# The first key group's convolution by halves of the batches between the gathers, and two gate blocks inside the sample's selected attention

## What is computed

```python
def compress(k, pe, w1, w2):                      # kcb, vcb: compressed blocks
    chunks = ...                                  # 16 tokens x 64 channels each
    pre = pe.reshape(-1) @ w1                     # position term
    for j in range(2):
        pre = pre + jnp.einsum('bngf,fh->bngh', chunks[:, j:j + n_cmp], w1r[j])
    return jax.nn.gelu(pre) @ w2

def merge_branches(o_nsa, o_hg, ga, gb, w_branch_a, w_branch_b, w_out):
    m = jax.nn.sigmoid(ga) * (o_nsa @ w_branch_a) + jax.nn.sigmoid(gb) * (o_hg @ w_branch_b)
    return m @ w_out

# sample: past = cache_cmp[page_table]; kcb, vcb = compress(past + new); top-16 blocks of 64 tokens are
# gathered from cache_sel for o_slc; o_win attends state_win and the new tokens; new_win_sample is
# state_win shifted by the 4 new tokens
```

## Time and profile before

| | |
|---|---|
| median of 3 runs | 1476.8 us (1475.82 to 1482.26) |
| the profiled execution | 1477.04 us, of it 1475.2 us span of the core |
| mean granted clock of TensorE | 0.954 |
| PE busy | 1292.9 us (88%), PEld 639.3 us (43%) |
| DVE, ACT, POOL busy | 397.5 us (27%), 257.1 us (17%), 32.1 us (2%) |
| chain that ended last, by engine | PE 64%, DMA 26%, DVE 3%, SPq 2% |
| convolution of 504 columns (L811), all | 56.8 us busy, 256 records |
| gate blocks (L1220), all | 67.8 us busy, 256 records |

### The profile page before, as it was taken

The page is one execution under the profiler, slowest core; times in us unless marked ns, Lnnn a source line. Parts: engine busy times, 40 slices in busy tenths (PEclk is TensorE's granted clock), DMA queues, the critical chain, the costliest instruction groups (busy, mean ns, idle before and its releaser), DMA issues.

```text
span 1475.2 us, 32485 instructions
## 1 busy us (share of the span) xinstructions
PE 1292.9 (88%) x14329; PEld 639.3 (43%) x14329; DVE 397.5 (27%) x991; ACT 257.1 (17%) x618; POOL 32.1 (2%) x50
## 2 busy tenths in 40 slices
PE   5899998799989978899999679999998669797685
PEld 4554555466767433344444224444443123242232
DVE  5320012458743551112121102121211011121012
ACT  5100005556520310001010001010100000000001
POOL 2000003100000000000000000000000000000000
PEclk9899999999999989899999989999999789899897
DMA  9985764224297999999999999699999999999996
GB/s 283 328 305 200 265 231 168 68 60 156 61 260 254 377 378 424 424 423 426 426 424 422 425 425 425 273 420 414 424 424 425 422 425 425 426 422 424 426 425 252
DMA packets 99043, 503.98 MB, mean 342 GB/s; under 512 B 9473, under 2 KB 38937, under 8 KB 63938
## 3 DMA queue, kind: packets, MB, share of 16 engines
q1 hardware_dynamic: 95234, 483.47, 82.4%
q0 software_dynamic: 3520, 18.90, 3.7%
q10 hardware_dynamic: 192, 0.13, 0.0%
HBM read 496.33 MB, written 10.31 MB: 343 GB/s over the span
## 4 chain that ended last, share of the span: by engine, by line
PE 64%; DMA 26%; DVE 3%; SPq 2%; ACT 2%; issue 1%; POOL 0%; DVEq 0%; ACTq 0%
PE psum L1444 18%; DMA arena<-in_w_up 12%; DMA arena<-in_w_down 11%; PE psum L1463 9%; PE psum L811 4%; PE psum L1220 3%; PE psum L1051 3%; PE psum L1052 3%; PE psum L1477 3%; PE psum L1416 2%; PE psum L1317 2%; PE psum L1430 2%; DMA arena<-in_cache_cmp,arena 2%; SPq L702 2%; PE psum L824 1%
## 5 line engine op out<-in xcount | busy, mean ns | idle before, releaser
L1444 PE MATMUL psum<-arena 128*32 128x512 f32 x3328 | 407.3, 637 | 110.3 <-DMA arena<-in_w_up 95.2
L1444 PEld LDWEIGHTS psum<-arena 128*32 128x32 f32 x3328 | 114.8, 113 | 371.2 <-issue 288.2
L2493 DVE TENSOR_SCALAR arena<-psum 128x256 f32<-128x256 f32 x52 | 22.2, 426 | 678.6 <-PE psum L1430 678.6
L1463 PE MATMUL psum<-arena 128*32 128x256 f32 x3328 | 192.7, 381 | 7.7 <-DMA arena<-in_w_down 7.7
L1463 PEld LDWEIGHTS psum<-arena 128*32 128x32 f32 x3328 | 101.6, 110 | 75.7 <-DMA arena<-in_w_down 12.8
L1880 ACT ACTIVATE arena<-arena 128x256 f32<-128x256 f32 x52 | 21.7, 418 | 572.7 <-DVE arena L2493 572.7
L1220 PE MATMUL psum<-arena 128*128 128x288 f32 x256 | 67.8, 410 | 3.5 <-DMA arena<-in_w_in 2.9
L1477 PE MATMUL psum<-arena 32*128 32x256 f32 x864 | 61.9, 399 | 1.1 <-ACT arena L1889 0.6
L811 PE MATMUL psum<-arena 64*128 64x504 f32 x256 | 56.8, 598 | 1.7 <-DVE arena L1959 1.7
L1430 PE MATMUL psum<-arena 32*32 32x512 f32 x416 | 57.6, 625 | 0.0
L1416 PE MATMUL psum<-arena 128*32 128x256 f32 x832 | 55.9, 386 | 0.0
(11 more groups left out here) (458 smaller groups left out, 1319.5 us busy)
## 6 DMA issues: line engine op xcount, KB each, us to landing
arena<-in_w_up SPq DMA_DIRECT2D x128, 2048.0 KB, 31.7
arena<-in_w_down SPq DMA_DIRECT2D x64, 2048.0 KB, 26.4
arena<-in_w_ada SPq DMA_DIRECT2D x12, 2048.0 KB, 11.3
arena<-in_w_in SPq DMA_DIRECT2D x6, 2048.0 KB, 12.0
arena<-in_w_in SPq DMA_DIRECT2D x16, 512.0 KB, 4.1
arena<-in_state_win SPq DMA_DIRECT2D x4, 1024.0 KB, 11.0
arena<-in_w_out SPq DMA_DIRECT2D x1, 4096.0 KB, 18.1
out<-in_state_win SPq DMA_DIRECT2D x1, 4064.0 KB
```

What stands on the lines that cost most here:

```text
L1444: last = mm(banks[0][32 * j:32 * j + SLOT].rearrange("p (h c) -> p h c", h=2), xcT[:, q % 2, q // 2], up_cols[n % R_][:, q % 2, j], start= ...
L1463: last = mm(banks[1][32 * j:32 * j + SLOT, 256:512], aT[:, v, 2 * m + h], down_cols[n % R_][:, h, v, j], start=m + v + h == 0, stop=m + v ...
```

## The change

1. `convolve` takes a range of batches. Banks 4 and 5 (`block_bank`) hold group 0; they are first written by two matmuls of `prow`, which is still zero at that point, so that all later ones accumulate. The transposes of a batch become `raw_to_kvT(b)`. Group 0's first 16 positions run for batches 0 to 3 between the transposes of batches 5, 6 and 7, then for batches 4 to 7, then positions 16 to 31 for all, and only then come the rows, the modulations 0 to 2 and the rest. The front modulations use banks 0 and 1.
2. The first 16 positions of `w1` are issued by ScalarE at the program's start, the others and `w2` by SP behind the prompt's rows; these wait for `landed[6]`. The first slab of `w_in` waits for the last front modulation's copy (`mod_v`).
3. Two gate blocks (`EARLY`) leave the planned part: block 0 stands in place of `keep_clock` ahead of the selected probabilities, block 1 in four pieces in the loop. They have banks 2 and 4 and buffers of their own and wait for `s_max`. ScalarE's tanh for them stand in the same part. Their columns of `w_in` are those of the last two blocks (`gate_column`), so that the planned blocks keep their columns. `INSIDE` is now blocks 2 to 11, at the same places among the prompt's steps, `LEFT` is 12 to 15.
4. SP issues the loads of blocks 0 and 1 when the window values are through (`pv_ps` 2). The loop over the later loads starts at block 2; the copy of `state_win` stands behind `load_gate(5)` as before.

```diff
+EARLY = 2
+def gate_column(j):
+    return (j - EARLY) % NGATE
...
+AHEAD = EARLY + len(INSIDE)
...
-            for v in range(2):
-                sp.dma_start(w1[DH * v:DH * v + DH], A["cmp_w1"][0, v].rearrange("(s d) h -> d s h", d=DH)).then_inc(S("ld_w1"), 16)
...
-            sp.wait_ge(S(landed[5]), 16)
+            sp.wait_ge(S(landed[6]), 16)
...
+            sp.wait_ge(S("ld_w1"), 32)
+            for v in range(2):
+                sp.dma_start(w1[DH * v:DH * v + DH, 16:32], block_weights(v)[:, 16:32]).then_inc(S("ld_w1"), 16)
...
+            def load_gate(j):
+                if j >= EARLY + 2:
+                    sp.wait_ge(S("gate_ps"), j - 1)
+                c0 = ZW + P * gate_column(j)
+                sp.dma_start(piece_of(j), w_in[:, c0:c0 + P].rearrange("(k p) c -> p k c", p=P)).then_inc(S(f"ld_gp{j % 2}"), 16)
+
+            sp.wait_ge(S("pv_ps"), 2)
+            for j in range(EARLY):
+                load_gate(j)
             sp.wait_ge(S("pv_ps"), 3)
...
-            for j in range(min(NGATE, len(INSIDE) + 2)):
+            for j in range(EARLY, min(NGATE, AHEAD + 2)):
                 load_gate(j)
                 if j == 5:
...
+            for v in range(2):
+                mm(block_bank(0, v)[:, 0:NB * NCMP], prow[0:32, v], ident[0:32, 0:1].broadcast_to([32, NB * NCMP]), start=True, stop=False)
+            for b in range(6):
+                raw_to_kvT(b)
+            for q in range(4):
+                pe.wait_ge(S(f"pair_out{q}"), 4)
+            pe.wait_ge(S("ld_w1"), 32)
+            convolve(0, 0, 8, 0, 4)
+            raw_to_kvT(6)
+            convolve(0, 8, 16, 0, 4)
+            raw_to_kvT(7)
...
-            pe.wait_ge(S("ld_w1"), 48)
-            convolve(0, 0, 16)
-            after(pe, "peT")
+            convolve(0, 0, 16, 4, NB)
+            pe.wait_ge(S("ld_w1"), 80)
+            convolve(0, 16, 32)
             for n in range(3):
                 rows_to_hT(n)
                 modulation(n)
-            convolve(0, 16, 32)
             position_terms()
...
-                if (what, n) == ("sel_p", 0):
-                    keep_clock(bank, 10)
...
+            pe.wait_ge(S("mod_v"), FRONT)
...
+            def early_gate(j, ks):
+                if ks[0] == 0:
+                    pe.wait_ge(S(f"ld_gp{j % 2}"), 16)
+                    pe.wait_ge(S("s_max"), 4)
+                for k in ks:
+                    last = mm(banks[2 + 2 * j][:, 0:TP + NS], piece_of(j)[:, k], hT[:, k], start=k == 0, stop=k == KD - 1)
...
+            early_gate(0, range(KD))
             for t in range(5):
                 probs_T("sel_p", t, 3)
+                if t < 4:
+                    early_gate(1, range(2 * t, 2 * t + 2))
                 if t:
                     cached_values("sel_p", t - 1)
...
+            for v in range(2):
+                act.dma_start(w1[DH * v:DH * v + DH, 0:16], block_weights(v)[:, 0:16]).then_inc(S("ld_w1"), 16)
...
             for t in range(5):
                 probs_out("sel_p", t, 2)
+            gates_out(0)
             act.wait_ge(S("pv_ps"), 3)
             nc.scalar.copy(o_ev[:, 0], banks[0][:, 0:P]).then_inc(S("oS"), 1)
+            gates_out(1)
```

More of the change, by code:

```diff
@@ L242 @@
 _end = max(n for n, s in enumerate(PROMPT_STEPS) if s[0] not in ("gates", "gates_out"))
-INSIDE = [j for j in range(NGATE) if PROMPT_STEPS.index(("gates_out", (j,))) < _end]
-LEFT = [j for j in range(NGATE) if j not in INSIDE]
+INSIDE = [j for j in range(EARLY, NGATE) if PROMPT_STEPS.index(("gates_out", (j,))) < _end]
+LEFT = [j for j in range(EARLY, NGATE) if j not in INSIDE]
+AHEAD = EARLY + len(INSIDE)
 PROMPT_STEPS = [s for s in PROMPT_STEPS if s[0] not in ("gates", "gates_out") or s[1][0] in INSIDE]
@@ L775, in rows_to_hT, with raw_to_kvT @@
                 last.then_inc(S("hT_ps"), 1)
-            for b in range(NB):
+            def raw_to_kvT(b):
                 pe.wait_ge(S(landed[b]), 16)
@@ L809, in convolve @@
                         half = slice(DH * v, DH * v + DH)
-                        src = kvT[half, g, s % 16].rearrange("p (b c) -> p b c", c=64)[:, :, s // 16:s // 16 + NCMP]
-                        last = mm(banks[2 * g + v][:, 0:NB * NCMP], w1[half, s], src, start=s == 0, stop=s == 31)
+                        src = kvT[half, g, s % 16].rearrange("p (b c) -> p b c", c=64)[:, b0:b1, s // 16:s // 16 + NCMP]
+                        last = mm(block_bank(g, v)[:, NCMP * b0:NCMP * b1], w1[half, s], src, start=g == 1 and s == 0, stop=s == 31)
                 if past == 32:
@@ L1219, in gate_block @@
                 for k in range(4 * half, 4 * half + 4):
-                    last = mm(banks[7][:, 0:TP + NS], gate_piece[j % 2][:, k], hT[:, k], start=k == 0, stop=k == KD - 1)
+                    last = mm(banks[7][:, 0:TP + NS], piece_of(j)[:, k], hT[:, k], start=k == 0, stop=k == KD - 1)
                 if half:
```

55 lines of the change are left out of this document (30 added, 25 removed).

## The result

The changed kernel takes 1488.97 us (median of 4 runs, 1486.62 to 1491.79) against 1476.45 us before: 12.5 us more; the ratio is 1.0089 (13.1 us) with a 95% interval of 1.0058 to 1.0120. The forecast was 1482.9 with a range up to 1488.5; the direction was right, the size was half of what came, and the time lies 0.5 us above the range. The profiled execution took 1486.6 us (span 1484.8) and is the shortest of the four, 9.6 us over the profiled one of before. The other 2.9 us lie between the profiled executions and the medians; the other three runs had a mean granted clock of 0.945 to 0.948, the profiled one 0.953, and where they lost it no trace here shows.

What follows compares the result with a forecast made beforehand. The expert-weight stream bounds the kernel and starts when the merged rows mT are done, so TensorE's path there counts. 1477.0-1.6-3.5+11.0 = 1482.9 us; own range 1479 to 1486.5, wider range 1474 to 1488.5.

Steps and rivals of the forecast that it cites:

- Part 2: Two early gate blocks at the selected softmax and its loop, two fewer behind the prompt: -3.5 us, bounds -6 and -1.
- Part 3: Copy of the window state issued two blocks earlier in the prompt's steps; TensorE waits for columns: +11.0 us, bounds 6.5 and 13.
- ScalarE's and VectorE's lead: During TensorE's wait behind the copy both run ahead, worth about 1 us of their later waits, bounds 0 and 3.
- Rival (a): Prompt's steps: the columns behind the copy don't wait for it, giving 1471.9 us; chance 0.11.
- the loads beside the last gather: Early gates' column loads issued beside batch 7's gather of selected rows: +0.3 us, bounds 0 and 3.
- The loop: Behind the selected softmax, second early block spread over it: 4.2 us less 0.32 us of waits, +3.9.
- the end: Behind the prompt: two blocks out, -8.4, most of 2.9 us waits gone, 1.4 left, +1.9 for VectorE's sums.
- new wait for VectorE's sums: Behind the prompt TensorE waits for eight sums of state that two fewer blocks no longer cover: +1.9 us.
- Part 1: Group 0's convolution in half records between the gathers' transposes: -4.1 at group 1, +2.5 clock, -1.6 us; bounds -6 and +4.
- rival (c): Convolution halves cost as much as whole records, stationary loads not hidden: +12.3, 1495.2 us; chance 0.05.
- rival (d): At the start batch 0 comes no earlier, with 0.14 us a half record: +3+2.6, 1488.5 us; chance 0.10.
- 4.1 us sooner at group 1: Group 1's convolution starts at 87.7 instead of 91.85 us, set by the last modulation slab landing at 85.2.

## Why the prediction was wrong

By the ratios the three parts alone are worth -3.4 us (the halves), +3.2 (the early gates) and +12.1 (the copy's place), together +11.9; the forecast had -1.6, -3.5 and +11.0, together +5.9. Part 2 is off by 6.7 us, about the whole miss.

**Part 3, the copy, was read rightly, and its size too, but for a wrong reason.** Forecast: the columns land 25.0 us after the copy's issue, TensorE stands 9.5 us. Measured: 339.0 + 17.8 - 331.95 = 24.9 us and 9.59 us. The clock behind it cost 1.7 us (3.86 against 2.18) instead of 2.5. The 1 us that ScalarE's and VectorE's lead was to give back did not come; TensorE was 0.4 us later instead. By the ratios the copy's place is worth 12 us in the changed kernel and 15.5 on the kernel before. Rival (a) asked whether the columns wait for the copy; they do, in whatever queue it is. Its ground, that the copy needs not all engines, was right, and half of the columns did pass at once; but a load has landed only when its last packet has.

**Part 2 failed at one step: the loads beside the last gather.** The forecast gave it 0.3 us with bounds 0 and 3, by the size of the packets. The gather took 7.6 us in the changed kernel and 9.1 in the early gates alone, against 6.1, so the wait grew by 1.5 and by 3.0 us, the upper bound; and the clock behind that wait, which I had worked out at the other two places, was left out here: 5.6 us for 16 records instead of 3.0. Together 4.1 us in the changed kernel's trace (1.5 and 2.6), 5.6 in that of the early gates alone, and 4.9 by the ratios with late loads against early ones. The loop came as forecast (3.8 - 0.4 = 3.4 us by the table, against 3.9). So did the end. From the block behind the copy to L1333 the table falls by 5.2 us; with 1.7 of clock and 0.4 behind that block taken out it is -7.3 against -7.7, with the new wait for VectorE's sums at 2.65 us. (The terms that the prediction lists for the end, -8.4, -2.9 + 1.4 and +1.9, give -8.0; the 0.3 us between is in no term.) The filler at half clock behind the loop added 2.6 us that no step had.

**Part 1 was wrong in its steps, and its sign right.** Halves at 0.115 us a record stand between 0.108 and the chosen 0.12; their weights took 187 ns as in the earlier trace rows, and rival (c) had no ground. The Trainium skill's lower value for them (TensorE: Matmul & The Clock Gate, section LDWEIGHTS; an estimate of 107 ns by the prediction) does not show here either. The start failed: I took the weights off the gathers' side, which gave 4.0 us (6.8 instead of 10.8 for the first gather), and put them ahead of the page table, which took 3.5, so batch 0 came at 14.88; that was half of rival (d). The zeros were free, as forecast: they ended at 14.75, and the gather landed at 14.9. Slab 3 was asked for at 70.5 instead of 66.5, and from there to the last slab's landing it was 20.4 us instead of 18.7; that the last slab sets the start of group 1 was right. The term "4.1 us sooner at group 1" was +1.5 in this trace; the four other traces with the same front have -0.7 to +0.5, so its sign isn't fixed, but 4.1 is in none. Yet the kernel with the halves alone is 3.4 us faster, of which 1.3 to 1.6 is likely the pause at 236 us that no step had. So the sign of part 1 came right by luck. It is luck too that the table shows a miss of only 1.7 us up to the probabilities: the profiled execution of before lost 2.7 us to a half clock at 232, where the three other traces with the old front lose 1.3 to 1.6 to the pause.

**The sum.** In the profiled executions +9.6 instead of +5.9: 1.7 up to the probabilities, -0.5 in the loop, 2.4 in the filler's stretch, -0.1 in the wait (9.59 less the 0.16 that stood there before), -0.8 for the clock behind it, 1.4 in the lead that wasn't paid back, 0.4 at the end of the gates and -0.8 behind. The range ended at 1488.5 because I had given each half-clock stretch a price only at places where I knew of a wait, and had added the parts' upper bounds nowhere (they give 1493). The clock's share of a wait belongs into every bound.

## What to carry to other kernels

When a program numbers its steps and a side job hangs on one number, look what the number means after the steps are renumbered: one unchanged `if j == 5` made 12 of the 12.5 us here. A big copy from DRAM to DRAM held up later small loads even from another queue, so put it where the next load isn't needed for as long as the copy takes. A wait on TensorE can cost its length and then a half clock behind it, and here a small load beside a gather that somebody waits for made such a wait; issued when the gather had landed, it cost nothing. And before a pause is called a wait for data, look in the code whether there is a wait at that instruction at all.

## What the runs showed of the hardware

- The copy of 4 MB delays a load of 0.5 MB issued 7 to 9 us after it so that it lands 25 to 26 us after the copy's issue, whether both are in SP's queue (24.9) or the copy is in ScalarE's (26.0), although the DMA engines' mean busy share was 0.56 in the stretch of the wait. The copy's 64 packets of 65 KB ran eight at a time, and half of the load's packets came only behind them:

```profile
347.30:356.80 9.50, 0.00 (x0) 0.00 (x0) 1.04 (x3) 2.13 (x10) 0.00 (x0) 0.64 0.56 194
```

- A transfer of 0.25 KB, the page table, issued 0.45 us after the first of two of 0.5 MB in another engine's queue, was cast 0.6 to 3.5 us later than without them, in six traces.
- A transfer of 0.5 MB issued while gathers were pending landed 20 to 22 us later, again from another queue than theirs.
- Behind waits of 2.85 and 4.36 us ahead of the last batch, the next two groups of 8 records took 1.97 and 3.62 us (clock 0.50); behind waits of 1.05 to 1.35 us at the same place 1.09 and 1.91 us. Behind the wait of 2.65 us at L1333 16 records took 4.13 us, the full clock.
- TensorE paused 0.7 to 3.5 us with no releaser in the profile, 22 times in fourteen traces, and each pause ended 1.3 to 1.6 us after a packet of 16 KB in the queue "instruction" had. The longest, 3.3 to 3.5 us, stood in the middle of a modulation.
- Two DMAs of 2 MB in pieces of 512 B held the engine that issued them for 12.85 us, and the next load's issue took 11.95 us, where the copy in large pieces had taken 0.82 and such a load 0.39.
